# A block-inverse recurrence on TensorE: one of four blocks computed in the half it comes from, and the bursts of two units issued as one interleaved stream

## The reference, cut to what matters

```python
def wkv7_scan(r, decay, k, v, kk, a):
    def step(S, inp):
        sa = jnp.einsum('bhij,bhj->bhi', S, -kk_t)
        S = (S * w_t[:, :, None, :]
             + sa[..., None] * (kk_t * a_t)[:, :, None, :]
             + v_t[..., None] * k_t[:, :, None, :])
        y = jnp.einsum('bhij,bhj->bhi', S, r_t)
        return S, y
...
def rwkv7_layer(h, ...):
    proj = token_shift(rmsnorm(h, norm) @ w_in, mu)     # r, k, v, z, two low ranks
    y = wkv7_scan(rh, decay, kh, vh, kk, a)
    out = (groupnorm(y) + bonus) * silu(z)
    return h + out @ w_out
```

## Time and profile before

| what | value |
|---|---|
| median of 3 runs | 2095.21 us (2095.17 to 2097.77) |
| the profiled execution | 2094.33 us, its span 2092.5 us |
| TensorE busy over the span | 1942.0 us (93%) |
| VectorE, ScalarE, GpSimd busy | 1005.3, 941.9, 303.3 us |
| granted TensorE clock, mean of the span | 0.972 |
| rounds with both halves and fill | about 130 to 1010 us of the span, 30 rounds |
| the four rounds of one pair, segment 0 to 3 | about 28.5 to 32 us each |

### The profile page before, as it was taken

One profiled execution on the slowest core, in us unless ns is written; L12 is line 12 of the kernel. 1 busy time (PEld: TensorE's weight loads), 2 busy tenths in 40 slices (PEclk: granted clock), 3 DMA queues, 4 the chain that ended last, 5 costly groups with the idle time before them and its releaser, 6 DMA issues.

```text
span 2092.5 us, 56861 instructions
## 1 busy us (share of the span) xinstructions
PE 1942.0 (93%) x24903; PEld 1673.3 (80%) x24903; DVE 1005.3 (48%) x1904; ACT 941.9 (45%) x1677; POOL 303.3 (14%) x317
## 2 busy tenths in 40 slices
PE   6699999999999999999789779999999999999798
PEld 4588888989898888989689577777787777777477
DVE  2645555556556555555633544334353344334521
ACT  2445454544545454544421344455536454455521
POOL 0013122221313122231000120001010110100000
PEclk9899999999999999999789898999999999999799
DMA  5101000010101000010322211011010111010233
GB/s 205 51 3 39 15 26 28 18 38 5 48 8 38 18 25 28 18 38 6 99 92 61 102 34 31 16 36 26 26 36 26 26 31 31 21 36 16 81 118 119
DMA packets 103739, 89.93 MB, mean 43 GB/s; under 512 B 4101, under 2 KB 95864, under 8 KB 103240
## 3 DMA queue, kind: packets, MB, share of 16 engines
q1 hardware_dynamic: 100120, 68.50, 11.1%
q0 software_dynamic: 3168, 17.14, 2.6%
q10 hardware_dynamic: 208, 0.66, 0.1%
HBM read 64.96 MB, written 21.33 MB: 41 GB/s over the span
## 4 chain that ended last, share of the span: by engine, by line
PE 78%; ACT 8%; DVE 7%; issue 4%; DMA 1%; POOL 1%; SPq 0%; ACTq 0%; DVEq 0%; POOLq 0%
PE ps L1734 7%; PE ps L2053 5%; PE ps L1735 5%; PE ps L1736 5%; PE ps L2055 5%; PE ps L2054 5%; PE ps L2136 5%; PE ps L1839 5%; PE ps L1669 3%; PE ps L1671 3%; PE ps L1670 3%; PE ps L1868 2%; PE ps L2089 2%; PE ps L1863 2%; PE ps L2117 2%
## 5 line engine op out<-in xcount | busy, mean ns | idle before, releaser
L1734 PE MATMUL ps<-xh,wh 128*128 128x258 f32 (+1 forms) x1024 | 322.4, 315 | 10.5 <-POOL wl L720 7.0
L1735 PE MATMUL ps<-xh,wl 128*128 128x258 f32 (+1 forms) x1024 | 291.1, 284 | 0.0
L1736 PE MATMUL ps<-xl,wh 128*128 128x258 f32 (+1 forms) x1024 | 290.9, 284 | 0.0
L2053 PE MATMUL ps<-xh,wh 128*128 128x348 f32 x744 | 254.0, 341 | 9.9 <-ACT arena_b L1092 6.6
L2054 PE MATMUL ps<-xh,wl 128*128 128x348 f32 x744 | 239.9, 323 | 0.0
L2055 PE MATMUL ps<-xl,wh 128*128 128x348 f32 x744 | 239.9, 322 | 0.0
L1734 PEld LDWEIGHTS ps<-xh,wh 128*128 128x128 f32 x1024 | 193.6, 189 | 27.7 <-issue 9.6
L1613 DVE TENSOR_REDUCE arena_b<-ps 128x1 f32<-128x144 f32 (+4 forms) x224 | 106.3, 506 | 191.5 <-PE ps L2093 176.5
L1735 PEld LDWEIGHTS ps<-xh,wl 128*128 128x128 f32 x1024 | 194.2, 190 | 1.7
L1736 PEld LDWEIGHTS ps<-xl,wh 128*128 128x128 f32 x1024 | 193.7, 189 | 0.0
L882 ACT ACTIVATE arena<-ps,pp 128x257 f32<-128x257 f32 (+1 forms) x128 | 61.2, 478 | 267.5 <-PE ps L1736 267.5
(11 more groups left out here) (262 smaller groups left out, 4471.4 us busy)
## 6 DMA issues: line engine op xcount, KB each, us to landing
wr<-in_w_in SPq DMA_DIRECT2D x33, 512.0 KB, 4.0
xt_scr<-arena POOLq DMA_DIRECT2D x2, 4176.0 KB, 13.4
wr<-in_kv_w SPq DMA_DIRECT2D x16, 512.0 KB, 3.9
wr<-in_b_w_in SPq DMA_DIRECT2D x16, 512.0 KB, 3.9
arena<-xt_scr SPq DMA_DIRECT2D x8, 522.0 KB, 4.6
arena<-oa_scr SPq DMA_DIRECT2D x8, 520.0 KB, 3.6
arena<-in_x SPq DMA_DIRECT2D x8, 512.0 KB, 3.4
wr<-in_w_out SPq DMA_DIRECT2D x8, 512.0 KB, 4.8
```

The lines of the kernel that those rows point to most:

```text
L1734: pe.matmul(bank, wh[:, j, k, :], xh[:, k, t], start=(k == 0), stop=False)
L1735: pe.matmul(bank, wl[:, j, k, :], xh[:, k, t], start=False, stop=False)
L1736: mm = pe.matmul(bank, wh[:, j, k, :], xl[:, k, t], start=False, stop=(k == KO - 1))
L2053: pe.matmul(bank[:, 0:SEG], wh[:, slot, k, :], xh[:, k, t], start=(k == 0), stop=False)
```

## The change

It does four things, all in the recurrence.

1. **One block in its own half.** `far(x, c)` gives the half in which the crossing operand of block x lies: the other half for blocks 1 and up, the own half for block 0. P (above level 0), XT of level 0 and X of block 0 thus become diagonal. So that the two kinds of quarter write different banks, block 0's P goes to the last 64 columns of bank 2 and the others to bank 3; X of block 0 and all XT go to bank 4, the other X to bank 5. P, now in a bank shared with transposes and `wu`, gets waits for those (`rows_ready`, `rp_ready`, `y0_ready`, and in `tr` and `wu_ready` for the mask of P).
2. **Two units' steps as one.** In rounds with both halves the steps of stage 2 to 5 become one step `px` each that interleaves crossing and diagonal products of both units, with all waits at its head; stage 1 becomes `px` of level 0 (P of level 0 with X step 3), and stage 6 becomes `wx` (wu with X step 2), in which X precedes and XT follows. Step p3 stays alone.
3. **Stage 0.** On TensorE `amat` now comes ahead of p3, not behind it. On VectorE the mask of p3 comes between the two parts of `amat`'s mask (step `amask`).
4. **Level 5's add.** VectorE did it in two operations of 64 partitions and all blocks; now it takes three: one of 128 partitions for block 0, and two of 64 partitions for the others.

The number of TensorE products is the same. The diff, cut:

```diff
-        B_SY, B_P, B_R, B_M, B_GA = 0, 1, (2, 3), (4, 5), (6, 7)
+        B_SY, B_R, B_P, B_M, B_GA = 0, (1, 2), 3, (4, 5), (6, 7)
+        XT_, X_ = 0, 1
+        AT_0 = 512 - CH
+        p_banks = ps[:, B_R[1]:B_P + 1, :].rearrange("p b c -> p (b c)")
+        x_banks = ps[:, B_M[0]:B_M[1] + 1, :].rearrange("p b c -> p (b c)")
...
+        def far(x, c):
+
+            return HALVES[c if x == 0 else 1 - c]
+
+        def p_cols(x, n=1):
+            return slice(AT_0 + x * CH, AT_0 + (x + n) * CH)
+
+        def xt_cols(nb, x, n=1):
+            return slice(AT_0 + (x - nb) * CH, AT_0 + (x - nb + n) * CH)
...
+        BOTH = [[], [("px", 0, 3)], [("px", 4, 0)], [("px", 1, 4)], [("px", 5, 1)], [("px", 2, 5)], [("wx",)], []]
...
-            steps = [("amat", (0,)), ("tr", (0,))] if early and s_ == 0 else []
+            steps = [("amat", (0,)), ("amask", (0,)), ("tr", (0,))] if early and s_ == 0 else []
             for i in range(8):
                 both = ((EARLY[i] if early else []), (LATE[i] if late else []))
+                if early and i == 0:
+                    steps += [("amat", (1, 2))]
+                if early and late:
+                    steps += BOTH[i]
                 for half in both if i % 2 else both[::-1]:
                     steps += half
                 if early and i == 0:
-                    steps += [("amat", (1, 2))]
+                    steps += [("amask", (1, 2))]
...
                         dve.wait_ge(S.a_done, n_a + 1)
-                        mask(0, CH).then_inc(S.ab_masked, 1)
-                        mask(CH, 4 * CH).then_inc(S.ar_masked, 1)
...
+                            dve.tensor_tensor(xs[:, X_, 0, :], got[:, XT_, 0, :], xs[:, XT_, 0, :], ALU.add)
                             for c, hc in enumerate(HALVES):
                                 hs = HALVES[1 - c]
-                                add = dve.tensor_tensor(xs[hc, 0, 0:nb, :], got[hs, 1], xs[hs, 1, 0:nb, :], ALU.add)
+                                add = dve.tensor_tensor(xs[hc, X_, 1:nb, :], got[hs, XT_, 1:nb, :], xs[hs, XT_, 1:nb, :],
+                                                        ALU.add)
...
+                def p_ready(l):
+
+                    pu, su = (early, late)[l // 3]
+                    if l == 0:
+                        pe.wait_ge(S.ab_masked, 5 * p + s_ + 2)
+                    elif l == 1:
+                        pe.wait_ge(P_MASKED[0], level(pu, su, 0) + 1)
+                    else:
+                        pe.wait_ge(X_COPIED[(l - 1) // 3], level(pu, su, l - 1) + 1)
+                    if l == 3 and not (isinstance(n1, int) and n1 < 1):
+                        for sem in (S.nd_ready, S.rp_ready, S.y0_ready):
+                            pe.wait_ge(sem, n1)
+                    elif l < 3 and has_late:
+                        pe.wait_ge(P_MASKED[1], level(*late, l) + 1)
+                    elif l > 3 and has_early:
+                        pe.wait_ge(P_MASKED[0], level(*early, l - 4) + 1)
+                    if l == 1 or l == 4 and has_early:
+                        pe.wait_ge(S.rows_ready, NT * p + 2 * s_ + 3)
+
+                def x_ready(l):
+
+                    h = l // 3
+                    pu, su = (early, late)[h]
+                    pe.wait_ge(P_MASKED[h], level(pu, su, l) + 1)
+                    if l == 1:
+                        pe.wait_ge(X_COPIED[0], level(pu, su, 0) + 1)
+                    if l == 3 and has_early:
+                        pe.wait_ge(S.ar_masked, 5 * p + s_ + 2)
+                    elif l > 3 and has_early:
+                        pe.wait_ge(X_COPIED[0], level(*early, l - 4) + 1)
+                    elif h == 0 and has_late:
+                        pe.wait_ge(X_COPIED[1], level(*late, l) + 1)
+
+                def wu_ready():
+
+                    pe.wait_ge(X_COPIED[1], level(*late, LEVELS - 1) + 1)
+                    pe.wait_ge(S.q_copied, n1 + 1)
+                    if has_early:
+                        pe.wait_ge(P_MASKED[0], level(*early, 2) + 1)
...
+                def p_block(l, block):
+
+                    x, j, e = block
+                    pu, su = (early, late)[l // 3]
+                    for c, hc in enumerate(HALVES):
+                        to = p_banks[far(x, c), p_cols(x)] if l else ps[hc, B_P, x * CH:(x + 1) * CH]
+                        mm = pe.matmul(to, am2[su % 2][hc, e, j, A_BA], xs2[su % 2][hc, X_, x, :] if l else ident[hc, hc],
+                                       start=(l > 0), stop=True, skip_group_check=True)
+                    return mm
...
+                def xt_block(l, block):
+
+                    x, h = block[0], l // 3
+                    pu, su = (early, late)[h]
+                    xs, pm, nb = xs2[su % 2], pm2[h], len(blocks(su))
+                    for c, hc in enumerate(HALVES):
+                        r = far(x, c)
+                        if l:
+                            mm = pe.matmul(x_banks[r, xt_cols(nb, x)], pm[r, x, :], xs[r, XT_, x, :], start=True, stop=True,
+                                           skip_group_check=True)
+                        else:
+                            mm = pe.matmul(x_banks[r, p_cols(x)], xs[hc, X_, x, :], ident[hc, hc], start=True, stop=True,
+                                           skip_group_check=True)
+                    return mm
+
+                def x_block(l, block):
+
+                    x, h = block[0], l // 3
+                    su = (early, late)[h][1]
+                    for c, hc in enumerate(HALVES):
+                        r = far(x, c)
+                        mm = pe.matmul(x_banks[hc, p_cols(x)], xs2[su % 2][r, XT_, x, :], pm2[h][r, x, :], start=True,
+                                       stop=True, skip_group_check=True)
+                    return mm
...
+                merged = has_early and has_late
...
+                    if merged and (kind in ("x", "q", "wu") or kind == "p" and st_[1] != 3):
+                        continue
...
+                            if i and has_late:
+                                pe.wait_ge(P_MASKED[1], level(*late, 3) + 1)
...
+                    elif kind == "px" and st_[1] == 0:
+
+                        l = st_[2]
+                        bp, bx = blocks(s_), blocks(late[1])
+                        p_ready(0)
+                        x_ready(l)
+                        p_seed(len(bp))
+                        for i in range(max(len(bp), len(bx) - 1)):
+                            if i + 1 < len(bx):
+                                x_block(l, bx[i + 1])
+                            if i < len(bp):
+                                mm = p_block(0, bp[i])
+                        mm.then_inc(P_DONE[0], 1)
+                        for b in bx:
+                            xt_block(l, b)
+                        x_block(l, bx[0]).then_inc(X_DONE[1], 1)
+                    elif kind == "px":
+
+                        lp, lx = st_[1:]
+                        hp, hx = lp // 3, lx // 3
+                        bp, bx = (blocks((early, late)[h][1]) for h in (hp, hx))
+                        whole, two = 0 < lx < LEVELS - 1, lx > 0
+                        p_ready(lp)
+                        x_ready(lx)
+                        if lx == 0:
+                            pe.wait_ge(S.ar_masked, 5 * p + s_ + 2)
+                            pe.wait_ge(S.rows_ready, NT * p + 2 * s_ + 3)
+                        pe.sem_inc(S.begun, 1)
+                        n_p, n_x = len(bp) - 1, len(bx) - 1 if lx < LEVELS - 1 else 0
+                        n_off, n_near = n_p + n_x, len(bx) + (2 if n_x else 1)
+                        for i in range(max(n_off, n_near)):
+                            if i < n_p:
+                                mm = p_block(lp, bp[i + 1])
+                                if i == n_p - 1:
+                                    mm.then_inc(P_DONE[hp], 1)
+                            elif i < n_off:
+                                b = bx[i - n_p + 1]
+                                mm = x_block(lx, b) if whole else xt_block(0, b)
+                                if i == n_off - 1 and n_off > n_near:
+                                    mm.then_inc(X_DONE[hx], 1)
+                            if i == 0:
+                                p_block(lp, bp[0])
+                            elif i <= len(bx):
+                                b = bx[i - 1]
+                                mm = xt_block(lx, b) if two else q_block(b)
+                                if i == len(bx) and not two:
+                                    mm.then_inc(S.q_done, 1)
+                                elif i == len(bx) and not n_x:
+                                    mm.then_inc(X_DONE[hx], 1)
+                            elif i < n_near:
+                                mm = x_block(lx, bx[0]) if whole else xt_block(0, bx[0])
+                                if n_off <= n_near:
+                                    mm.then_inc(X_DONE[hx], 1)
+                    elif kind == "wx":
```

(35 more changed lines are left out.)

115 lines of the change are left out of this document (36 added, 79 removed).

## The result

The changed kernel takes 2071.43 us (median of 4 runs, 2070.05 to 2072.91), the kernel before, measured beside it, 2095.49 us (4 runs, 2095.17 to 2097.77). The ratio is 0.988, 95% interval 0.987 to 0.990: faster by 24 us, where 20.7 were forecast. The profiled execution of after took 2071.86 us with a span of 2070.0, 22.5 us less than before by either measure.

What follows compares the result with a forecast made beforehand. TensorE was taken to bound the recurrence. Per-round gains of 0.78, 0.69, 0.70 and 0.59 us in segments 0 to 3, over 7, 8, 8 and 7 rounds, made 20.7 us: 2095.2 to 2074.5 us, range 2067 to 2088.

Steps and rivals of the forecast that it cites:

- slot model: TensorE bursts: the longer of crossing and diagonal kinds sets the length, one slot being 0.058 us; 4-block round -0.80 us.
- reach of three slots: TensorE records pass each other only within three slots, so a kind listed behind the other starts three slots before its end.
- slower rival: Mixed bursts run two records a slot, not four abreast; a round 2.2 us longer, 2161 us in all; chance 0.08.
- Merged waits: Rival: merged steps start the next burst late, four stages of 30 rounds losing 0.1 us each, 2086.5 us; chance 0.12.
- (a): Level-5 add ahead of wu takes 0.12 us more on VectorE; +0.10, +0.16, 0.27 us lost in segments 2, 1, 0.
- (b): Segment 3, projection behind stage 5: its wait for POOL grows by 0.16 us, and stage 0's 0.05 goes too.
- (c): Stage 0 of segment 0: p3 behind amat comes 0.40 us later, not 0.05 earlier, so +0.45 us a round.
- Stage 0 in segments 1 and 2: p3 goes from 8 to 6 crossing slots but stands behind amat; -0.05 us in a 4-block round.
- Rounds put at 0: The round without fill, waiting for VectorE and ACT, and the first and last rounds, with one half, change by 0.
- first rival: More comes through: three adds cost no more than two, 4.0 us, and p3 hides as before, 3.2 more; 2067.5; chance 0.13.

Runs made afterwards that it cites:

- own half alone: The changed kernel with block 0 in its own half, three adds and p3 behind amat, but each unit's steps issued apart as before; 2087.01 us, ratio 0.997.
- The merge alone: The changed kernel with all blocks crossing again and level 5's add in two operations, the two units' steps still merged; 2081.48 us, ratio 0.994.
- wu_one_wait: The changed kernel with the wait for q moved to stage 5, leaving one semaphore instruction between the level-5 add and wu; 2068.47 us, ratio 0.988.

## Why the prediction was right, step by step

- **The slot model held.** Stages of a round with 4 blocks, from first record to projection: 0.98, 1.32, 0.86, 0.74, 1.33 and 1.62 us for stages 2, 3, 4, 5, 1 and 6, where 0.98, 1.34, 0.87, 0.75, 1.34 and 1.62 were forecast. The reach of three slots held too: with the own half alone, q stands in the listing behind 12 crossing slots, starts three before their end, and with the chain makes 19 slots, 1.10 us, where 1.12 were measured.
- **The slower rival fell.** A mixed burst of 48 records takes 0.71 us from first to last start (stage 4 in a round of segment 2); the bound was 0.75. Bursts that mix P, q and XT run four abreast as X and XT do. By the rule in the Trainium skill, "TensorE: Matmul & The Clock Gate", section "Wait — 56ns, not 53.3ns?", starts are never under about 25 ns apart, and by an estimate from it this burst would need 1.2 us. The trace disagrees, with 47 distances in 0.71 us, 15 ns each.
- **Merged waits don't show.** L1816, which heads the merged steps, waited 3.9 us in three places, all of them ahead of 155 us or behind 985 us, in the first and last rounds. All other bursts start 0.21 us behind the last projection, as before.
- **(a) Right in effect, wrong in cause.** The forecast was +0.10, +0.16 and +0.27 us in segments 2, 1 and 0, some 4 us in all, and `wu` came later by 0.08, 0.14 and 0.24, which makes 3.4. That the distances match is partly luck, for the step that held the third operation to cost 0.12 us is wrong. The timeline of DVE, mask of p2, then the adds, against the earlier trace rows:

```profile
291.13 0.41 DVE L1456 TENSOR_TENSOR arena<-ps,levels 128x256 f32<-128x256 f32 x1
291.46 0.21 DVE L1471 TENSOR_TENSOR arena<-ps,arena 128x64 f32<-128x64 f32 x1
291.69 0.72 DVE L1474 TENSOR_TENSOR arena<-ps,arena 64x192 f32<-64x192 f32 x2
```

  From the start of the mask to the end of the adds it is 292.41 - 291.13 = 1.28 us. Before, the mask started at 294.98 in the same view and the adds ended at 296.29, so it was 1.31. The new operation lasts 0.21 us, not the 0.28 of the earlier trace rows, and overlaps the mask by 0.08. The merge alone, with two adds, takes 1.31 too, and its `wu` is late; the own half alone, with three, isn't late. What took the place of the third add is a second semaphore instruction of TensorE ahead of the merged step. The rest of the step was right: the shorter stage 5 moves the last projection, not the adds, so their end comes 0.04 us behind its start in segment 2, where before it came 0.11 ahead. The prediction counted the merged waits at nothing because their inputs are early. It didn't count that a wait which is over still takes time to issue when the queue behind it is empty.
- **(b)** Right for the 0.16: POOL's waits rose from 1.0 to 1.16 us. The 0.05 of stage 0 wasn't there to lose, and segment 3 gained 0.06 more than forecast.
- **(c)** Right mechanism, 0.34 instead of 0.40 us a round against p3 in its old place, and `amat` waits 1.1 us, not 0.9: with p3 no longer ahead of it, it loses p3's whole stretch.
- **Stage 0 in segments 1 and 2** was put at -0.05 and is up to 0.16 us longer in segment 2 (1.61 against 1.44 us from first to last small record), for the same missed term: `amat`'s three semaphore instructions stood behind p3's 16 records before and were hidden by them. Now they stand behind four records of the chain. With two of the three gone, a round of segment 2 is 0.22 us shorter, which would leave some -0.05, as forecast.
- **Rounds put at 0.** Over the 29 rounds from the first `mm` burst on, single rounds ran long, more so before (31.83 and 31.44 us for 31.07, among others) than after; the difference is 1.37 us beyond what the medians say. The last two rounds take 0.34 us longer after than before, and what lies behind them 1.15 us less. So 20.4 + 1.37 - 0.34 + 1.15 make the 22.5 us between the spans within 0.1. Whether the 1.37 and the 1.15 belong to the change is open. The further 1.6 us up to the difference of the medians is within what runs of one kernel differ.

The sum over the filled rounds, 20.4 us for the 20.7 forecast, came so near partly since errors cancelled: segments 1 and 2 gained 0.05 and 0.10 us a round less than reckoned, segments 0 and 3 gained 0.07 and 0.06 more. Against the 24 us between the medians it is 3 us short. Three sums of the prediction are slightly off, and nothing hangs on them: its terms for segment 2 add up to -0.81, not -0.80; the low end of the first rival is 2067.3; and the slots that it gives for the slower rival add up to 33 more, not 38, so some 57 us and 2152.

## What to carry to other kernels

Where an engine is the bound and its records overlap, count the distances between starts and write down the rule by which they run side by side; busy time would have shown nothing here. Count the semaphore instructions of a merged or moved step, not only when their inputs are ready: what is free behind sixteen queued records costs 0.1 us each behind four or at a wait that binds. And look at the waits that are left (here POOL's in segment 3): taking that one away was worth 8 us by the medians on either kernel, a third of what the change itself gave.

## What the runs showed of the hardware that was not expected

- A semaphore instruction in TensorE's queue costs 0.105 to 0.11 us when nothing is queued ahead that hides it: 271.785, 271.896, 272.007 in after. Two of them fewer were worth 0.22 us. With two behind each other at a wait that binds, the first record came 0.25 us behind the end of VectorE's adds (after, segments 0 and 2); with one it came 0.10 behind (`wu_one_wait`, segment 0).
- Records on different quarters of the array start 15 ns apart on average over a burst of 48, when they come from different steps and write different banks of PSUM. Two kinds of quarter in the same bank weren't tried.
- A VectorE operation of 128 x 64 can start 0.08 us before the end that the profile gives for the one ahead of it, so an extra short operation cost less than its own length: from the mask to the end of the adds it is 1.28 us with three adds and 1.31 with two.
